# Tile 0 of a product-key expert layer gives 32 instead of 16 of its tokens to gathered rows

## What is computed

```python
def peer_ffn(xn, w_query, sub_keys, u, v):
    def one_block(xb):                              # 128 tokens
        q = (xb @ w_query).reshape(BLOCK, PEER_HEADS, 2, PEER_HALF)
        s = jnp.einsum('thcd,hckd->thck', q, sub_keys)
        ...                                         # 8 heads x 16 best of 16384 experts
        g = jax.nn.softmax(top_s.astype(jnp.float32), axis=-1)
        ue = jnp.take(u, expert, axis=0)
        ve = jnp.take(v, expert, axis=0)
        act = jax.nn.gelu(jnp.einsum('thkd,td->thk', ue, xb), approximate=False)
        return jnp.einsum('thk,thkd->td', g * act, ve)
```

## Time and profile before

| what | value |
|---|---|
| median of 3 runs | 1751.37 us (1748.77 to 1754.53) |
| the profiled execution, its own time | 1754.55 us |
| its span, first to last instruction | 1752.8 us |
| TensorE (PE) busy | 1681.0 us, 96% |
| VectorE (DVE) busy | 1338.6 us, 76% |
| ScalarE (ACT) busy | 694.2 us, 40% |
| GpSimd (POOL) busy | 727.9 us, 42% |
| mean granted TensorE clock | 0.983 |
| moved by DMA | 442.46 MB, mean 252 GB/s |

### The profile page before, as it was taken

How to read it: one execution, slowest core, us unless ns; L and a number is a source line. 1 busy time by engine, 2 the same in 40 slices (tenths; PEclk the granted TensorE clock), 3 DMA queues, 4 the chain that set the end, 5 groups by cost and what they waited for, 6 DMA issues and landing times.

```text
span 1752.8 us, 27510 instructions
## 1 busy us (share of the span) xinstructions
PE 1681.0 (96%) x10039; PEld 1499.9 (86%) x10039; DVE 1338.6 (76%) x3072; ACT 694.2 (40%) x1039; POOL 727.9 (42%) x510
## 2 busy tenths in 40 slices
PE   7999998989889999999999999999999999999998
PEld 6778776555656679989999999999999999999998
DVE  5574954757678777999999923985798888888886
ACT  5333335242323323446446634653333333333332
POOL 5243340000000466877777776777372222222220
PEclk9999998999999999999999999999999999999999
DMA  4122213444443787789999998998999999999993
GB/s 165 44 96 73 96 49 120 148 141 154 135 155 134 245 316 256 254 281 324 327 339 302 317 379 320 349 339 295 401 385 344 331 345 330 344 333 341 342 330 119
DMA packets 158791, 442.46 MB, mean 252 GB/s; under 512 B 15824, under 2 KB 50256, under 8 KB 155360
## 3 DMA queue, kind: packets, MB, share of 16 engines
q1 hardware_dynamic: 117040, 290.04, 46.8%
q0 software_dynamic: 41472, 151.01, 23.9%
q10 hardware_dynamic: 176, 0.07, 0.0%
HBM read 399.12 MB, written 41.94 MB: 252 GB/s over the span
## 4 chain that ended last, share of the span: by engine, by line
PE 69%; DVE 6%; DMA 3%; ACT 2%; issue 1%; POOL 1%; DVEq 0%; ACTq 0%
PE psum L2199 29%; PE psum L1316 7%; PE psum L1317 7%; PE psum L1318 7%; PE psum L1246 6%; PE psum L1345 3%; PE psum L1233 3%; DMA u<-in_u 3%; PE psum L1146 2%; POOL ul L1597 1%; DVE psum L1847 1%; PE psum L1202 1%; PE psum L1180 1%; ACT probs L1458 1%; DVE hits L1883 1%
## 5 line engine op out<-in xcount | busy, mean ns | idle before, releaser
L1597 POOL TENSOR_TENSOR ul<-u,uh 128x1024 fp32r<-128x1024 f32 x128 | 315.1, 2469 | 395.9 <-ACT uh L1505 394.3
L1316 PE MATMUL psum<-split,uh 128*128 128x368 f32 x1024 | 349.9, 342 | 7.1 <-POOL ul L1597 5.4
L2199 PE MATMUL psum<-wh,vl 128*128 128x368 f32 x1024 | 338.7, 331 | 0.0
L1317 PE MATMUL psum<-split,uh 128*128 128x368 f32 x1024 | 337.6, 330 | 0.0
L1318 PE MATMUL psum<-split,ul 128*128 128x368 f32 x1024 | 337.4, 329 | 0.0
L2172 POOL DMA_INDIRECT v_row<-in_v,tri x128 | 148.6, 1161 | 334.8 <-DVE mixed L2271 327.6
L1316 PEld LDWEIGHTS psum<-split,uh 128*128 128x128 f32 x1024 | 193.2, 189 | 11.9 <-POOL ul L1597 8.1
L1317 PEld LDWEIGHTS psum<-split,uh 128*128 128x128 f32 x1024 | 193.5, 189 | 1.4 <-issue 1.4
L1318 PEld LDWEIGHTS psum<-split,ul 128*128 128x128 f32 x1024 | 193.0, 188 | 0.0
L2199 PEld LDWEIGHTS psum<-wh,vl 128*128 128x128 f32 x1024 | 192.3, 188 | 0.0
L1505 ACT CAST uh<-u 128x1024 fp32r<-128x1024 f32 x128 | 133.8, 1047 | 131.4 <-DMA u<-in_u 131.2
(11 more groups left out here) (341 smaller groups left out, 3264.5 us busy)
## 6 DMA issues: line engine op xcount, KB each, us to landing
u<-in_u SPq DMA_DIRECT2D x128, 512.0 KB, 5.9
v<-in_v SPq DMA_DIRECT2D x64, 1024.0 KB, 5.1
act_mat<-act_w SPq DMA_DIRECT2D x128, 184.0 KB, 6.0
w<-act_mat SPq DMA_DIRECT2D x64, 368.0 KB, 7.5
wraw<-in_w_wide SPq DMA_DIRECT2D x18, 1024.0 KB, 5.1
w_low<-in_w_branch_b SPq DMA_DIRECT2D x8, 1024.0 KB, 5.3
w_high<-in_w_branch_a SPq DMA_DIRECT2D x8, 1024.0 KB, 5.5
w_low<-in_w_out SPq DMA_DIRECT2D x8, 1024.0 KB, 5.2
```

The source lines that it names most:

```text
L1316: nc.tensor.matmul(out, high[:, c], dense_x[0][:, c], start=(c == 0), stop=False)
L1317: nc.tensor.matmul(out, high[:, c], dense_x[1][:, c], start=False, stop=False)
L1597: nc.gpsimd.tensor_tensor(ul[:, n % U_COLS], u[:, n % U_COLS], uh[:, n % UH_COLS].bitcast(F32), ALU.subtract).then_inc(s["u_low"], 1)
L2199: mm = nc.tensor.matmul(bank(m, c)[:, 0:WIDTH], lhs, rhs, start=first and k == 0 and p == 0, stop=final and p == 2)
```

## The change

`EXTRA` is 32: the last 32 tokens of tile 0 leave the dense products, with four groups of picks to a token instead of eight. `TOKENS` becomes 96, 128, 128 and `WIDTH` 352. There are 32 gathers of u and 32 of v for the extra tokens, with 32 dots and 32 mixes, at new places of the tables. Tile 0's groups are 24 instead of 28 (6 pairs of columns instead of 7), and start 20 pairs of columns in instead of 16.

```diff
-EXTRA = 16
+EXTRA = 32
 EXTRA_GROUPS = P // EXTRA
 EXTRA_RING = 4
 TOKENS = [P - EXTRA, P, P]
...
-EXTRA_DOTS_BEFORE = {NT * UNITS + 7: 4, NT * UNITS + 9: 4}
-EXTRA_DOTS_BEHIND = {NT * UNITS + 13: 4, NT * UNITS + 14: 4}
-EXTRA_GATHERS_AT = {3: 4, 6: 4, 7: 4, 11: 4, 12: 4, 15: 2, 17: 2, 19: 2, 21: 2, 23: 2, 25: 2}
-EXTRA_MIXES_AT = (2, 2, 2, 2, 2, 2, 2, 2)
+EXTRA_DOTS_BEFORE = {NT * UNITS + at: 4 for at in (5, 7, 8, 9, 10)}
+EXTRA_DOTS_BEHIND = {NT * UNITS + at: 4 for at in (12, 13, 14)}
+EXTRA_GATHERS_AT = {n: 4 for n in (3, 4, 6, 7, 8, 9, 11, 12, 13)} | {n: 2 - (n % 3 == 0) for n in range(17, 34)}
+EXTRA_MIXES_AT = (4, 4, 4, 4, 4, 4, 4, 4)
...
-AHEAD = (0, 16, 9, 9)
+AHEAD = (0, 20, 9, 9)
```

## The result

The changed kernel takes **1761.17 us** (median of 4 runs, 1760.39 to 1765.51) against 1751.66 for the kernel before on the same chip (1748.77 to 1754.53): ratio 1.0061, 95% interval 1.0039 to 1.0082. It is slower by about 9.5 us. The forecast was 1744 and its range ended at 1760, so both the sign and the range were wrong. The profiled execution is the slowest of the four (1765.51, span 1763.7), 4 us above their median; in the work ahead of step 48, where nothing was changed, it is 2.4 us behind the profiled execution of before. (Over all kernels of this document that unchanged part takes 565.0 to 575.8 us, so that stages are compared by their lengths and not by where they lie.)

A forecast was written before the change was run, and what follows sets the result against it. It took TensorE, 69% of the chain that ended last, to bound the kernel. Its terms, -22.1 - 12.4 - 0.4 - 3.0 + 7.2 + 13.5 - 4.0 + 13.4 + 0.6 = -7.2 us, gave 1744, range 1729 to 1760.

The forecast's parts named there:

- Last products: Final stage: 3072 matmuls each 7.2 ns shorter, -22.1 us, if the other engines keep up.
- (C): Rival, last products: DMA engines become the bound, a column takes 3.96 us instead of 3.85, total 1758.7; chance 0.14.
- (E): Rival, all matmuls: they do not get shorter with the width, 34.9 us stays away, total 1779; chance 0.02.
- +0.6 for the start: Start of the last products: no lead any more on VectorE, +0.6 us.
- Plain columns, -12.4: First products: 84 plain columns save 14.5 us, less doubt about DMA in 18 of them, -12.4 us.
- Row in step 59, +7.2: Tile 3's `row` in step 59: there at about 647, so TensorE waits 7.2 us for it.
- Gates columns and two fewer of them: Gates columns: 88 groups stay at VectorE's pace, -0.4 us; two columns fewer spare 1.48 each, -3.0 us.
- POOL and `chosen(2)`, +13.5: Routing to hand-over: POOL full and mixes waiting for gathers make TensorE wait before columns 22 to 32, +13.5 us.
- hand-over -4.0: Last plain column to tile 0's first group: 5.3 us instead of 9.3, -4.0 us.
- Rival (B): Waits at step 59 and column 31 hardly come: 2 and 4 instead of 7.2 and 13.5, total 1729.5; chance 0.20.
- Tail, +13.4: Last group to first last product: 48 us, 17.2 above the columns instead of 3.8, +13.4 us.

The follow-up runs named there:

- ahead_alone: Kernel before with the first group of gates 19 pairs of columns behind the first plain one instead of 16, all else the same: 1758.13 us, ratio 1.0031.
- short_chosen: Changed kernel with the eight dots inside the search for tile 2's picks computed over 64 columns instead of 1024: 1754.21 us, ratio 1.0006.
- dots_to_gap: Changed kernel with four of the eight dots in tile 2's search moved between tile 2's and tile 3's pairs of groups: 1758.00 us, ratio 1.0029.
- ring_of_8: Changed kernel with eight buffers instead of four for gathered v rows, and four of these gathers two to three columns earlier: 1750.25 us, ratio 0.9976.

## Why the prediction was wrong

*Last products.* By the starts of the matmuls the pitch is 160.2 ns after and 167.8 before, 7.6 less where 7.2 were taken, and TensorE met no DMA limit at 350 GB/s, so rivals (C) and (E) fell. (The prediction's 167.3 is 100 us over 598, a count that takes in matmuls reaching over the edges.) In the 100 us from 1260 the engines moved 389 GB/s; the figure of about 358 that the prediction quoted from the Trainium skill (SBUF — State Buffer, "A bandwidth-pool intuition that's wrong") is passed again, and the measurement decides. The stage still gave 17.1, not 21.5: the "+0.6 for the start" was mis-sized, and 6.0 is what it measured. A wait for VectorE's split comes in the first 20 us, and behind the start and behind that wait some ten matmuls each start every 0.29 us instead of 0.16, at a granted clock of 0.50 and 0.52 (1257.5 to 1260.4, the last row below with its columns as in the busy times above, and 1277.6 to 1281):

```profile
1257.45 0.63 PE L2199 MATMUL psum<-wh,vh_first 128*128 128x352 f32 x1 [3.31 <-DVE wl L2257]
...
1277.49 0.41 PE L2199 MATMUL psum<-wh,vh_first 128*128 128x352 f32 x1 [2.98 <-DVE wl L2257]
```

```profile
1257.50:1260.40 2.90, 2.90 (x10) 2.90 (x11) 2.86 (x7) 0.49 (x1) 2.29 (x3) 0.50 0.99 334
```

The first wait lies ahead of the first last product and belongs to the tail. 7.6 ns by 3072 are 23.3 us; less 3.1 for the second wait and 2.9 for the slow matmuls that makes 17.3. The kernel before has none of this, and `ahead_alone`, with its short tail and the old width, has it too (531.2 us against 523.3): it comes with the later gates and the short tail, not with the width.

*Plain columns, -12.4.* **This step failed.** It priced 84 columns by TensorE's pitch and doubted only DMA. In the 18 columns of tile 2's search VectorE has no idle time to speak of, and they got 4.6 us longer; `short_chosen` and `dots_to_gap` show VectorE as the cause. The busy shares had been there to read: VectorE worked 76.7 of the 80 us in which TensorE worked 79.4.

Why the stage grew even beyond 76.4 can be read from where VectorE begins the search. Before:

```profile
840.62 3.19 DVE L1774 MAX8 val<-s_sb 128x8 f32<-128x128 f32 x16
...
842.49 0.84 PE L1345 MATMUL psum<-hot 128*128 128x128 bf16 x12
```

and after:

```profile
878.98 0.84 PE L1345 MATMUL psum<-hot 128*128 128x128 bf16 x12
...
879.98 3.18 DVE L1774 MAX8 val<-s_sb 128x8 f32<-128x128 f32 x16
```

Before, VectorE began 1.9 us ahead of TensorE's last group of tile 0; after, 1.0 us behind it. These 2.9 us are most of the 4.6. (The stage is counted from TensorE's last group.) The prediction had not seen this lead: it took TensorE's group at 798.65 for the one that VectorE had ready at 798.46. Counted through, that group of VectorE's is the one TensorE takes up at 801.39, and VectorE is 2.9 us ahead from the fourth group of tile 0 on. In the changed kernel TensorE takes each group up 0.06 us behind VectorE from the seventh group on, so that nothing of the lead is left, and in `ahead_alone` 0.8 is left. Part of it comes back in the groups, which took 12.5 us less instead of 11.1.

The remaining 1.7 us are VectorE's own. The sum of its tensor operations, copies and casts in the stage is 36.4 us before, 39.3 after and 39.6 in `ahead_alone`, the same 46 instructions, and its idle time fell from 2.7 to 1.6. Single groups of them move much further, both ways (busy, mean ns, idle). Before:

```profile
L1881 DVE TENSOR_TENSOR hits<-top_at_f,iota 128x1600 f32<-128x1600 f32 x2 | 9.0, 4509 | 0.0
...
L1791 DVE TENSOR_TENSOR code<-idx_f 128x64 f32<-128x64 f32 x3 | 0.7, 221 | 0.0
```

and after:

```profile
L1791 DVE TENSOR_TENSOR code<-idx_f 128x64 f32<-128x64 f32 x3 | 5.6, 1861 | 0.0
...
L1881 DVE TENSOR_TENSOR hits<-top_at_f,iota 128x1600 f32<-128x1600 f32 x2 | 4.2, 2086 | 0.0
```

Where nothing is in the way, such a `code` takes 0.22 us and such a `hits` 1.8. In these rows one `code` of 5.17 us (from 911.95) lies beside two subtractions of POOL (912.26 to 917.02), and before one `hits` of 6.62 us (from 895.89) beside three (893.70 to 900.82). Which of them meets a subtraction changes with every shift of the columns against the search; that this makes the remaining 1.7 us is argued from these rows, not shown.

*Row in step 59, +7.2.* **The wait was right, the size was not.** `row` was expected to be there at 647 and was at 654.7; 2.4 of these 7.7 us lie ahead of step 48. `stream`'s second half came 12.9 us later than before, where the term had 4.6 for four more dots. The 12.9 are the 2.4, another 2.1 by which VectorE came late to step 56's work, the four dots with their waits for landings, 6.4, and 2.1 by which a `hits` took longer (3.90 us instead of 1.82, beside a subtraction of POOL). And the term left out the engine in between: ScalarE takes the square sum in order ahead of column 5's GELU. In all the stage lost 12.6 us against columns alone, 5.4 more than the term.

*Gates columns and two fewer of them* came as said: 2.73 us a group, VectorE's pace. Tile 2's groups lost 4.0 us in the profiled execution, with 5.9 us of waits for a `stage` copy of ScalarE, the longer of which in turn stood behind a landing of `u`. In the other kernels with 352 columns and 32 extra tokens these waits are 1.2 to 3.6 us, and the kernel before had 1.8; so this is about the one execution more than about the change.

*POOL and `chosen(2)`, +13.5, hand-over -4.0.* Right to 0.6 us in the sum, and the hand-over to the tenth: 811.26 to 816.56. The places are less right. TensorE's waits for POOL come before columns 22 to 33 and make 9.9 us, with slower columns behind them 13.5. The longest is 3.3 before column 29, as said; before column 31, where 7.7 had been counted, it is 1.2, and 1.6 and 1.7 follow before columns 32 and 33. That the single waits add up to the forecast is therefore luck in part. The reason was right: POOL stood 2.7 us at a gather for a mix ahead of the subtractions for columns 29 and 31, and in `ring_of_8` the same work with more buffers and four earlier gathers costs 10.9 us less, so it was not POOL's work alone. Rival (B) fell.

*Tail, +13.4.* Too high by 4: 43.7 us instead of 48, of which 3.3 are the wait in front of the first last product.

The forecast's error is therefore not in the large term but in three stages, 7.7, 5.4 and 4.4 us, where a shorter column was entered as gained, or a wait as small, because TensorE was the busiest engine there and the lead of VectorE was not counted. The tail gave 4.3 back.

## What to carry to other kernels

Before a matmul's saving is multiplied by a count, split the count by stage and look for stages in which another engine is nearly as busy as TensorE (76.7 against 79.4 us here); in this one the gain was nothing. Ask too what lead that engine brings into the stage, pairing its operations with TensorE's by counting them, since a lead that the change uses up is paid in the next stage. When work is added to a chain that several engines pass on (VectorE, ScalarE, VectorE, TensorE), follow the in-order queue of each engine in it, not only that of the one that gets the work. And when a change is slower than its two halves added, look stage by stage, in more than one execution, and at the resources that both use before giving it up: here four more buffers and a dozen dots in other places turned +9.5 us into -8.4.

## What the runs showed of the hardware

A VectorE operation on 128x1 took 5.10 and 5.17 us instead of 0.16, and one of 0.75 us took 5.29, each time until POOL's pair of subtractions (4.64) was through. The Trainium skill (SBUF — State Buffer, "Who interferes with whom") says that VectorE and GpSimd lock a pair of ports exclusively, for operations of VectorE with two inputs in SBUF and for its fast copy-like forms. The traces agree on both forms. On who goes first they settle nothing: by the page the operation that starts first holds the pair, and here the VectorE operation's recorded start (638.54) lies ahead of POOL's first subtraction (638.97), but POOL was in the issue of a gather (638.01 to 638.95) and began its subtraction 0.02 us behind it. What the rows do show is that VectorE isn't let in between two subtractions of POOL that follow each other: it waited out two here and, in the kernel before, the rest of one and two more (6.62 us). The prediction priced VectorE's operations at their undisturbed lengths and had no term for this.
